# Attention scores over all 128 rows, with each key head in a tile of its own whose other 64 rows are zero

## What is computed

```python
s = jnp.einsum('bqkgd,bskd->bkgqs', qblk, k)   # 64 features are summed over
p = jax.nn.softmax(s, axis=-1)
return jnp.einsum('bkgqs,bskd->bqkgd', p, v)
```

## Time and profile before

| | |
|---|---|
| median of 3 runs | 1971.09 us (1969.82 to 1972.81) |
| span of the profiled execution | 1973.0 us |
| its own time beside the runs | the span is 1.9 us above their median |
| PE busy | 1951.1 us, 99% |
| PE weight loads busy | 1660.6 us, 84% |
| DVE, ACT, POOL busy | 1642.5, 977.3, 838.5 us |
| `w_in` projection | to about 100 us |
| transposes of keys and queries, pooling mixer, attention | about 100 to 212.5 us |
| `w_out` and expert layer | from 212.5 us |

### The profile page before, as it was taken

The page is one execution under the profiler, slowest core; times in us unless marked ns, Lnnn a source line. Parts: engine busy times, 40 slices in busy tenths (PEclk is TensorE's granted clock), DMA queues, the critical chain, the costliest instruction groups (busy, mean ns, idle before and its releaser), DMA issues.

```text
span 1973.0 us, 28846 instructions
## 1 busy us (share of the span) xinstructions
PE 1951.1 (99%) x10204; PEld 1660.6 (84%) x10204; DVE 1642.5 (83%) x3148; ACT 977.3 (50%) x2043; POOL 838.5 (42%) x588
## 2 busy tenths in 40 slices
PE   8999999999999999999999999999999999999999
PEld 8977998987888888888888888788888888788887
DVE  3866436879999999999977776898988999889898
ACT  4266243324787787787877772332222222223231
POOL 0334102001333333433455655555666566666563
PEclk9999999999999999999999999999999999999999
DMA  6110312225789989989899999999999999999996
GB/s 267 43 36 1 139 54 107 79 88 196 232 301 326 300 311 311 321 296 303 299 378 397 401 411 406 362 343 406 390 405 388 407 401 406 399 407 404 406 399 256
DMA packets 203366, 581.27 MB, mean 295 GB/s; under 512 B 19936, under 2 KB 57184, under 8 KB 201056
## 3 DMA queue, kind: packets, MB, share of 16 engines
q0 software_dynamic: 73728, 268.47, 36.6%
q1 hardware_dynamic: 60192, 180.12, 24.5%
q10 hardware_dynamic: 69312, 130.97, 17.6%
HBM read 505.03 MB, written 74.45 MB: 294 GB/s over the span
## 4 chain that ended last, share of the span: by engine, by line
PE 63%; DMA 17%; DVE 11%; issue 4%; POOL 2%; ACT 2%; SPq 0%; ACTq 0%; DVEq 0%
PE ps L334 19%; PE ps L335 18%; PE ps L336 18%; DMA ring_a<-in_v,expert_ids 7%; PE ps L1516 5%; DMA ring_b<-in_v,expert_ids 5%; DVE sparse L1191 2%; DMA ring_c<-in_v,expert_ids 2%; DMA gel_dram<-arena_b 1%; PE ps L1390 1%; DVE arena_a L1215 1%; DVE v_lo_slots_b L1203 1%; POOL ring_c L833 1%; PE ps L1477 1%; DVE v_lo_slots_a L1203 1%
## 5 line engine op out<-in xcount | busy, mean ns | idle before, releaser
L334 PE MATMUL ps<-v_hi_slots,w_lo 128*128 128x512 f32 x1024 | 399.2, 390 | 2.5 <-DVE w_lo L1221 2.3
L336 PE MATMUL ps<-v_hi_slots,w_lo 128*128 128x512 f32 x1024 | 398.4, 389 | 0.0
L334 PE MATMUL ps<-feat_hi,w_hi 128*128 128x512 f32 (+1 forms) x936 | 360.1, 385 | 1.5 <-DVE w_lo L1093 1.1
L335 PE MATMUL ps<-feat_lo,w_hi 128*128 128x512 f32 (+1 forms) x936 | 351.2, 375 | 0.0
L336 PE MATMUL ps<-feat_hi,w_lo 128*128 128x512 f32 (+1 forms) x936 | 351.0, 375 | 0.0
L722 ACT ACTIVATE w_lo<-arena_a 128x512 fp32r<-128x512 f32 x128 | 81.0, 633 | 493.6 <-DVE arena_a L1215 371.4
L833 POOL DMA_INDIRECT ring_a<-in_u_rows,expert_ids x86 | 123.2, 1432 | 320.4 <-DVE ring_a L1183 186.1
L334 PEld LDWEIGHTS ps<-v_hi_slots,w_lo 128*128 128x128 f32 x1024 | 192.2, 188 | 45.0 <-DVE w_lo L1221 5.3
L336 PEld LDWEIGHTS ps<-v_hi_slots,w_lo 128*128 128x128 f32 x1024 | 192.2, 188 | 40.2
L336 PEld LDWEIGHTS ps<-feat_hi,w_lo 128*128 128x128 f32 x936 | 176.2, 188 | 31.8
L334 PEld LDWEIGHTS ps<-feat_hi,w_hi 128*128 128x128 f32 x936 | 176.6, 189 | 30.9 <-DVE w_lo L1093 1.9
(11 more groups left out here) (223 smaller groups left out, 4469.5 us busy)
## 6 DMA issues: line engine op xcount, KB each, us to landing
arena_a<-in_v ACTq DMA_DIRECT2D x121, 512.0 KB, 7.7
w_raw<-in_uT SPq DMA_DIRECT2D x85, 512.0 KB, 6.5
g_dram<-arena_a ACTq DMA_DIRECT2D x64, 512.0 KB, 8.4
gel_dram<-arena_b ACTq DMA_DIRECT2D x120, 256.0 KB, 5.4
w_raw<-gel_dram SPq DMA_DIRECT2D x120, 256.0 KB, 8.2
arena_a<-in_uT SPq DMA_DIRECT2D x43, 512.0 KB, 6.8
w_raw<-in_w_all SPq DMA_DIRECT2D x16, 1024.0 KB, 5.8
arena_b<-g_dram SPq DMA_DIRECT2D x32, 512.0 KB, 11.8
```

What stands on the lines that cost most here:

```text
L334: nc.tensor.matmul(out, lh, rh, start=first, stop=False)
L335: nc.tensor.matmul(out, lh, rl, start=False, stop=False)
L336: return nc.tensor.matmul(out, ll, rh, start=False, stop=last)
```

## The change

The keys go to a new tile, `keys_padded`, at words 2048 to 5119 of `arena_a`: high and low part, each with a block of 768 tokens for key head 0 (features on partitions 0 to 63, zeros on 64 to 127) and one for key head 1 (zeros on 0 to 63). POOL fills the zeros with two instructions once `var1` is there. ACT's two copies of the keys become four, over 64 partitions each, and DVE's two subtractions four. `scores` takes all 128 partitions of the query tile and of the head's key block, in three matmuls as before: the queries of the other head meet zeros. PE waits for `zero_k` once ahead of the first scores.

```diff
+        KP_ = at("keys_padded", 24576 + 2048, 3072, F32R)
-        kTh, kTl = KV_[:, 0:TOK], KV_[:, TOK:2 * TOK]
+        k_padded = view(KP_, 0, 2, 2, TOK)
@@ ACT
             def flip_out(r):
                 act.wait_ge(qk_tr, r + 1)
-                dst, b, ok = (kTh, 6, k_hi) if r == 0 else (FTh[:, r - 1, :], 6 - 2 * (r % 2), q_hi)
-                nc.scalar.activation(dst[:, 0:512], ps[:, b, :], ACT.Copy).then_inc(ok, 1)
-                nc.scalar.activation(dst[:, 512:768], ps[:, b + 1, 0:256], ACT.Copy).then_inc(ok, 1)
+                if r == 0:
+                    for b, c in ((0, 512), (1, 256)):
+                        for hh in range(2):
+                            rows = slice(64 * hh, 64 * hh + 64)
+                            nc.scalar.activation(k_padded[rows, 0, hh, b * 512:b * 512 + c], ps[rows, 6 + b, 0:c],
+                                                 ACT.Copy).then_inc(k_hi, 1)
+                    return
+                dst, b = FTh[:, r - 1, :], 6 - 2 * (r % 2)
+                nc.scalar.activation(dst[:, 0:512], ps[:, b, :], ACT.Copy).then_inc(q_hi, 1)
+                nc.scalar.activation(dst[:, 512:768], ps[:, b + 1, 0:256], ACT.Copy).then_inc(q_hi, 1)
@@ POOL
+            pool.wait_ge(var1, 1)
+            nc.gpsimd.memset(k_padded[64:P, :, 0, :].bitcast(F32), 0.0).then_inc(zero_k, 1)
+            nc.gpsimd.memset(k_padded[0:64, :, 1, :].bitcast(F32), 0.0).then_inc(zero_k, 1)
+            pool.wait_ge(zero_k, 2)
@@ DVE
-                dve.wait_ge(k_hi, b + 1)
-                tt(kTl[:, b * 512:b * 512 + c], ps[:, 6 + b, 0:c], kTh[:, b * 512:b * 512 + c].bitcast(F32),
-                   ALU.subtract).then_inc(k_lo, 1)
+                dve.wait_ge(k_hi, 2 * b + 2)
+                for hh in range(2):
+                    rows, cols = slice(64 * hh, 64 * hh + 64), slice(b * 512, b * 512 + c)
+                    tt(k_padded[rows, 1, hh, cols], ps[rows, 6 + b, 0:c], k_padded[rows, 0, hh, cols].bitcast(F32),
+                       ALU.subtract).then_inc(k_lo, 1)
@@ PE (in flip_qk and ahead of the scores, k_lo is now awaited at 4)
+            pe.wait_ge(zero_k, 2)
@@ PE, scores
-                rows, cols = slice(64 * hh, 64 * hh + 64), slice((t0 + t) * P, (t0 + t + 1) * P)
-                keys = slice(t0 * P, (t0 + n) * P)
+                cols, keys = slice((t0 + t) * P, (t0 + t + 1) * P), slice(t0 * P, (t0 + n) * P)
                 pe.wait_ge(exp_ok, j * NU + (u + 1))
-                pe_split_product(ps[:, u % 3, 0:n * P], FTh[rows, j, cols], FTl[rows, j, cols], kTh[rows, keys],
-                                 kTl[rows, keys], True, True).then_inc(qk_mm, 1)
+                pe_split_product(ps[:, u % 3, 0:n * P], FTh[:, j, cols], FTl[:, j, cols], k_padded[:, 0, hh, keys],
+                                 k_padded[:, 1, hh, keys], True, True).then_inc(qk_mm, 1)
```

More of the change, by code:

```diff
@@ L282, in build @@
             sem(n) for n in ("a_mul", "a_hi", "a_lo", "v_hi", "v_lo", "a_mm", "acc_done", "acc_ev", "done"))
-        dve_step, zero_v = sem("dve_step"), sem("zero_v")
+        dve_step, zero_v, zero_k = sem("dve_step"), sem("zero_v"), sem("zero_k")
         y_tiles = (4, 5, 0, 1, 2, 3)
@@ L1347, in flip_qk @@
                 if r == 2:
-                    pe.wait_ge(k_lo, 2)
+                    pe.wait_ge(k_lo, 4)
                 elif r >= 3:
```

## The result

The changed kernel takes 1959.5 us (1958.54 to 1964.85, 4 runs) against 1970.8 of the kernel before: a ratio of 0.994, 95% interval 0.9928 to 0.9952, or 11.3 us less where 13.7 were forecast. Timed again beside the experiments it was 1959.6 against 1972.5, ratio 0.9935 (0.9921 to 0.9948). The profiled execution spans 1957.6 us, 15.4 less than the one of before; that is more than the runs differ, so the traces have to be compared stretch by stretch and not by their ends.

What follows compares the result with a forecast made beforehand. PE's order of work was taken to bound the attention stretch. Visits saved 15.2 us, less 1.5 for ACT waits, 0 for copies and 0 for fills: 13.7 off 1971.1 gives 1957.4 us, range 1952.5 to 1963.0.

Steps and rivals of the forecast that it cites:

- The price of a visit: Attention scores: going into and out of 64-row matmuls costs PE 0.33 us, 46 times, 15.2 us saved; bounds 6.0 and 18.4.
- The control in the expert stage: Eight 128-column matmuls and a 512-wide one took 1.13 us against 1.10 summed, so 0.03 came off the 0.36 price.
- the drain and the exposed load: Attention: changing row count drains TensorE and leaves a weight load unhidden; if only the drain went, 0.13 a visit.
- Rows, not wait, type or bank: Attention: the number of rows causes the price; score units in a row step by 0.23 us despite waits and another bank.
- The waits for ACT: Attention: faster PE waits for ACT's exponential at three score units, 0.5 us a pair, 1.5 us lost; bounds 0 and 3.
- The keys' copies: Four copies on ACT and four subtractions on DVE, covered by DVE's 2.78 us idle: cost nothing; uncovered 2.0 us.
- The fills: POOL's two zero fills, 2.8 us together, start beside DVE's short newton steps: cost taken as 0; upper bound 2.8 us.
- The rival of the exposed load: Attention: the drain goes but weight loads stay unhidden; gain 46 x 0.13 = 6.0 us, 1965.1 us; chance 0.07.
- ACT's order as the bound: Attention: waits for ACT go through the pair and half the gain is given back; gain 7 us, 1964; chance 0.10.
- no gain: Attention: the price hangs on changing operands between transposes, values and scores, and stays; 1971 us; chance 0.04.
- slower: Attention: faster PE stands waiting, its clock falls to half, one pair costs more than the gain; 1975.5 us; chance 0.02.
- The sign that I gave for a fall: Attention: PE's clock falls where a wait nears 1.9 us; the longest wait foreseen was some 0.3.

Runs made afterwards that it cites:

- e3: Changed kernel plus loops of matmuls on zeros over 64, 128 or alternating rows ahead of the first product; one execution, 2029.4 us.
- e1: Changed kernel with score matmuls reading only their head's 64 rows of the padded tile; 1974.4 us against 1972.5 of the kernel before, ratio 1.0011.
- e2: Changed kernel with key head 1's score units over 64 rows, key head 0's over 128; 1966.9 us against 1972.5 of the kernel before, ratio 0.9975.
- e4: The changed kernel run again, nothing altered; 1959.6 us against 1972.5 of the kernel before, ratio 0.9935.
- e8: Changed kernel with fills waiting for rstd1_ok and the first-batch output copy one step later; 1957.9 us against 1971.5 of the kernel before, ratio 0.9926.
- e5: Changed kernel with POOL's two fills waiting for rstd1_ok instead of var1; 1958.4 us against 1971.5 of the kernel before, ratio 0.9935.

## Why the prediction was right

*The price of a visit: right, in place, mechanism and size.* 0.33 us forecast, 0.34 measured by itself (e3), 0.33 from the account. The control in the expert stage that took 0.03 off my sums was worth it. The upper bound of 0.40 a visit and the lower of 0.13 both fall with e3. What is shown of the mechanism is that the change of rows costs it. What I called the drain and the exposed load can't be told apart by these runs; together they are 0.17 a change in a visit, and 0.20 where rows change at each matmul.

*Rows, not wait, type or bank: right* (e1, e3). That a visit costs the same between any neighbours, which let me multiply by 46, holds roughly (e2).

*The waits for ACT: right in mechanism and place, too small.* The step that was short is the second of the sum: 0.5 us a pair, 1.5 in all, was 2.3. I read the first of the three units from rows and guessed the other two. The rows give even less than the 0.2 that I wrote, 172.84 - 172.74 = 0.1, and the one shown cost 0.34, because PE gained more than I counted. In the kernel before, the last values matmul ahead of the unit is

```profile
171.39 0.28 PE L336 MATMUL ps<-w_hi,keys_values 128*128 128x256 f32 x1
```

and the unit follows at 173.07, 1.68 us later. After, the same way is 163.99 to 164.81 and 0.35 more, 1.17 without the wait: 0.51 sooner, not 0.33, since the part of the next visit's price that stands ahead of its first matmul (0.17) is gone too. The exponential is out 1.45 us behind the values matmul before (172.84) and 1.46 after (165.45), and 1.46 - 1.17 and the 0.05 until PE follows make the 0.34. In each pair two units waited, not three, by 0.30 to 0.34 us, and one in the first block, 0.31 us, where no output is copied; that one the prediction didn't have.

*The keys' copies: right at nothing.* DVE's four subtractions took 2.31 us, from 106.52 to 108.83, and PE went through its sequence at the old distances: `windows(0)` at 101.22 and the last transposes of the queries at 117.98, each 0.39 behind the kernel before. DVE in order of time, against the earlier trace rows:

```profile
106.52 2.31 DVE L957 TENSOR_TENSOR keys_padded<-ps,keys_padded 64x512 fp32r<-64x512 f32 x4 [1.07 <-ACT keys_padded L558]
...
110.64 1.14 DVE L939 SCALAR_TENSOR_TENSOR feat_lo<-ps,vecs,feat_hi 128x512 fp32r<-128x512 f32 x2 [0.76 <-ACT feat_hi L549]
```

The idle time of 2.78 us ahead of the mixer's step had shrunk to 0.76: that was the cover.

*The fills: wrong at nothing.* They cost 0.4 us, inside the bound. The row that I leaned on, a reciprocal of one column beside POOL, is another kind of step. The sign that I had set for it, the start at 29.37 unmoved, failed by 0.37 us. The rule that I set beside it, of the Trainium skill (SBUF — State Buffer, Who interferes with whom), named the right kind: single-source steps in a two-port mode wait for a GpSimd write, steps with two inputs don't. The trace agrees: the TENSOR_SCALAR waited, the TENSOR_TENSOR steps at 27.86 and 28.06 did not. The reciprocal at 27.64, single-source as well, took its usual 0.19 beside the fill, so being single-source is not enough; the section's list of steps that can wait (copy, cast, tensor_scalar) doesn't name it.

*The rival of the exposed load: fallen.* The rule of the Trainium skill (TensorE: Matmul & The Clock Gate, Part 3), by which a load overlaps a matmul in flight only where the row groups differ, doesn't hold in these traces: with 128 rows on both sides the transition costs nothing (0.79 us where 0.78 is the plain sum). The same section also lets a load run ahead where it goes to the background weight buffer, and with that the trace is in line.

*ACT's order as the bound, no gain, slower: none came.* The clock stood at 1.00 through the attention, 124 to 196 us. The sign that I gave for a fall, a wait near 1.9 us, is no good sign: in e4 the clock stayed up behind a wait of 2.5 us, and elsewhere it fell behind two of 1.1 and 1.3 (see the end).

With e3's price the sum is 15.6 - 2.3 - 0.4 = 12.9, the traces have 12.3, and the forecast was 13.7; the measured medians are 11.3 and 12.9 less.

## What to carry to other kernels

Going to matmuls over 64 rows between others over 128 costs 0.34 us a visit, in and out, as much as one and a half 512-wide matmuls here. Padding the operands with zeros to 128 rows saves it where such matmuls come a few at a time and the zeros can be written off the path; look for a first matmul that is 0.1 us longer than its neighbours and for idle time of the weight loads behind it. When the busiest engine is made faster, look through the order written for the others: here one output copy stood a step too early, which cost nothing before and 2.3 us after. A fill in POOL's unused time can cost something where a short step of DVE on the path is beside it: here one of four was held up.

## What was not expected

**The clock falls at the same place in some executions and not in others.** PE waits 1.6 to 2.5 us ahead of its start at 29.3 to 29.8. Of the nine traces of full executions without added work (before, after, e1, e2, e4 to e8) seven have the clock at half for some 3 us behind that wait, and e4 and e5 have none. Stretches by time of the changed kernel, and of e4, which is the same kernel:

```profile
31.00:33.00 2.00, 2.00 (x11) 2.00 (x11) 0.00 (x0) 2.00 (x2) 0.00 (x0) 0.50 0.97 376
```

```profile
31.00:33.00 2.00, 2.00 (x19) 2.00 (x19) 0.00 (x0) 2.00 (x3) 0.00 (x0) 1.00 0.94 363
```

19 matmuls in 2 us for 11. The last values matmul of e4 is at 198.5 where the changed kernel's other trace has 199.9: 1.4 us of pure luck, over three times what the fills cost. At a second place, in the expert stage, where PE waits 1.1 and 1.3 us for DVE, the clock fell in five of the nine traces (changed kernel, e1, e2, e4, e5) and not in the others, the kernel before among them:

```profile
470.00:474.00 4.00, 3.92 (x11) 3.09 (x12) 3.90 (x19) 0.00 (x0) 0.00 (x0) 0.61 0.60 159
```

In the kernel before the stretch behind these waits, 482 to 486 us, is at 1.00. So the 12.3 us of gain at the end of the attention are 10.6 behind this place (the same matmul, with `w_raw`, starts at 645.41 before and 634.77 after) and 11.6 where the last stage begins (1268.2 and 1256.6). A difference of a microsecond between two single traces is so no evidence for an edit until the clock has been compared.

**The clock fell with next to no idle time of PE.** In e3, where 64 and 128 rows took turns matmul by matmul from 24.12 on, it fell 4 us later, and it stayed at half through all the turns that followed, to 51 us. It fell again at 62 us, in the rounds of three matmuls over 64 rows and four over 128, which are the visits of the attention at one in every 1.48 us. Stretches by time, and PE in order of time at the fall:

```profile
26.00:27.00 1.00, 1.00 (x3) 0.40 (x3) 0.00 (x0) 0.00 (x0) 0.00 (x0) 1.00 0.80 336
27.00:37.00 10.00, 10.00 (x16) 4.07 (x15) 0.00 (x0) 0.00 (x0) 0.00 (x0) 0.54 0.88 318
...
56.00:62.00 6.00, 5.94 (x30) 3.93 (x28) 0.00 (x0) 0.00 (x0) 0.00 (x0) 1.00 0.00 0
62.00:72.00 10.00, 10.00 (x28) 6.53 (x27) 0.00 (x0) 0.00 (x0) 0.00 (x0) 0.50 0.01 2
```

```profile
27.57 0.55 PE L1330 MATMUL ps<-keys_values 64*128 64x512 f32 x1
28.05 0.79 PE L1331 MATMUL ps<-keys_values 128*128 128x512 f32 x1
28.77 0.79 PE L1330 MATMUL ps<-keys_values 64*128 64x512 f32 x1
```

0.72 us a matmul at half clock for 0.43 at full. In the attention of the kernel before, with a visit in every 1.9 us, it stayed at 1.00. So denser changes of rows than in this attention can cost the clock as well as their own price. The blocks of e3 that don't change rows kept the clock from 9 to 24 us, or got it back (51 to 56 us, and at 79 us). Why it fell isn't shown, all of this is one execution on zeros, and it was not tried in a kernel.

**Two halves side by side.** An estimate from e3: by L1325 and L1326 two score units of different key heads at the same time would take 0.23 us a step for both, and share one visit, 3 x 0.23 + 0.34 = 1.03 us for two 512-wide units, where the padded ones take 6 x 0.23 = 1.38. The three banks for scores and the order of the pipeline are in the way; it was not tried.
